# One layer of sparse attention and retention: values with v as stationary operand, gate projected transposed

## What is computed

```
u = rms_norm(x, norm_gain);  z = u @ w_in        # q k v gate of attention, index q k w, q k v gate of retention
score[t,s] = sum_h w_i[t,h] * relu(q_i[t,h] . k_i[s])      # causal; each query keeps its top 128 keys
p   = softmax(q_a . k_a / 8 over the kept keys)            # 8 heads of 64
y_a = (p @ v_a) * silu(g_a)
y_r = rms_norm_per_head(retention(q_r, k_r, v_r)) * silu(g_r)   # 4 heads, qk 64, v 128, chunks of 128
out = rms_norm(x + concat(y_a, y_r) @ w_out, final_gain)
```

## Time and profile before

| | us |
|---|---|
| median of three runs | 293.16 (292.93 to 293.17) |
| the profiled execution | 292.49 |
| its span from first to last instruction | 290.7 |

### The profile page before, as it was taken

One profiled execution on the slowest core, in us unless ns is written; L12 is line 12 of the kernel. 1 busy time (PEld: TensorE's weight loads), 2 busy tenths in 40 slices (PEclk: granted clock), 3 DMA queues, 4 the chain that ended last, 5 costly groups with the idle time before them and its releaser, 6 DMA issues.

```text
span 290.7 us, 4404 instructions
## 1 busy us (share of the span) xinstructions
PE 281.1 (97%) x1506; PEld 239.9 (83%) x1506; DVE 203.8 (70%) x414; ACT 142.8 (49%) x305; POOL 65.9 (23%) x122
## 2 busy tenths in 40 slices
PE   8999999999999999999999999999999999999991
PEld 7997888888888788877888888888888888888891
DVE  3967779999999999999956555658734733863341
ACT  5957646516455324582468442593444563341231
POOL 1016822132200068792400103011020020000211
PEclk9999999999999999999999999999999999999998
DMA  7998504210422043051303220212200407311123
GB/s 287 410 400 269 144 3 143 75 45 31 144 73 74 14 146 114 17 144 55 94 10 135 74 72 0 98 48 73 76 0 2 144 0 256 107 36 38 72 97 121
DMA packets 13845, 30.10 MB, mean 104 GB/s; under 512 B 1152, under 2 KB 1664, under 8 KB 13824
## 3 DMA queue, kind: packets, MB, share of 16 engines
q1 hardware_dynamic: 13248, 29.04, 30.3%
q10 hardware_dynamic: 576, 0.79, 0.7%
HBM read 27.73 MB, written 2.10 MB: 103 GB/s over the span
## 4 chain that ended last, share of the span: by engine, by line
PE 65%; DVE 20%; DMA 5%; issue 4%; POOL 2%; ACT 2%; SPq 2%; DVEq 0%; POOLq 0%; ACTq 0%
PE bank L441 16%; PE bank L443 15%; PE bank L442 15%; PE bank L492 6%; DVE keys L1079 6%; DVE top L1077 5%; DMA w_raw<-in_w_in 5%; DVE w_lo L978 3%; PE bank L506 3%; DVE keys L1064 2%; PE bank L521 2%; PE bank L522 2%; DVE k_stack L1040 2%; PE bank L531 1%; PE bank L552 1%
## 5 line engine op out<-in xcount | busy, mean ns | idle before, releaser
L441 PE MATMUL bank<-w_hi,xT_hi 128*128 128x512 f32 (+1 forms) x296 | 116.5, 394 | 0.6 <-DVE w_lo L978 0.5
L443 PE MATMUL bank<-w_hi,xT_lo 128*128 128x512 f32 (+1 forms) x296 | 114.1, 385 | 0.0
L442 PE MATMUL bank<-w_lo,xT_hi 128*128 128x512 f32 (+1 forms) x296 | 113.8, 384 | 0.0
L441 PEld LDWEIGHTS bank<-w_hi,xT_hi 128*128 128x128 f32 x296 | 55.7, 188 | 11.7 <-DVE w_lo L978 1.4
L443 PEld LDWEIGHTS bank<-w_hi,xT_lo 128*128 128x128 f32 x296 | 55.6, 188 | 11.5
L442 PEld LDWEIGHTS bank<-w_lo,xT_hi 128*128 128x128 f32 x296 | 55.7, 188 | 9.9
L978 DVE TENSOR_TENSOR w_lo<-w_raw,w_hi 128x1024 fp32r<-128x1024 f32 x36 | 45.2, 1276 | 16.3 <-ACT w_hi L622 16.1
L622 ACT ACTIVATE w_hi<-w_raw 128x1024 fp32r<-128x1024 f32 x36 | 37.4, 1053 | 5.7 <-PE bank L443 3.4
L737 ACT ACTIVATE work<-work,small 128x128 f32<-128x128 f32 (+3 forms) x32 | 17.8, 556 | 33.4 <-DVE small L1102 33.3
L1077 DVE MAX8 top<-keys 128x8 f32<-128x256 f32 (+2 forms) x48 | 26.9, 560 | 1.3
L916 POOL TENSOR_TENSOR th<-zt,tab 128x64 f32<-128x64 f32 (+1 forms) x24 | 13.1, 544 | 57.9 <-ACT zt L666 57.6
(11 more groups left out here) (130 smaller groups left out, 377.8 us busy)
## 6 DMA issues: line engine op xcount, KB each, us to landing
w_raw<-in_w_in SPq DMA_DIRECT2D x28, 512.0 KB, 3.8
w_raw<-in_w_out SPq DMA_DIRECT2D x8, 512.0 KB, 3.7
retT<-in_x SPq DMA_DIRECT2D x8, 256.0 KB, 3.7
x_h<-in_first SPq DMA_DIRECT2D x2, 836.0 KB, 7.8
out<-x_h SPq DMA_DIRECT2D x4, 320.0 KB, 2.5
v_ret<-in_x SPq DMA_DIRECT2D x2, 512.0 KB, 11.4
v_att<-in_x SPq DMA_DIRECT2D x2, 512.0 KB, 10.0
mix<-in_first SPq DMA_DIRECT2D x1, 836.0 KB, 5.4
```

Source lines behind the costliest of these rows:

```text
L441: pe.matmul(o, xh, hi[:, kk, c0:c0 + w], start=first, stop=False)
L442: pe.matmul(o, xh, lo[:, kk, c0:c0 + w], start=False, stop=False)
L443: mm = pe.matmul(o, xl, hi[:, kk, c0:c0 + w], start=False, stop=last)
```

## The change

- `values` takes v as the weights (64 columns) and the transposed probabilities as the moving operand (128 columns). The two heads of a pair go into partitions 0 to 63 and 64 to 127 of the bank, alternating for each key tile. Its result is y transposed.
- As the division by the sum can then no longer be made per row of the result, it is made on the probabilities: `reciprocal(s)` on VectorE for each pair, and `scale_probs(s)`, two copies with a scale on ScalarE. `transpose_probs(s)` waits for these.
- The chunks of the two gates change places: the gate of attention is now steps 24 to 27, that of retention 28 to 31.
- The gate of attention is projected transposed, with weights and x exchanged as operands, so its token factor is needed along the columns: `half_rstd` is spread by GpSimd, turned by four transposes in step 15 (`turn_rstd`) and copied by ScalarE. `att_z` multiplies it in on VectorE ahead of the tanh; `att_gate` makes the gate after the maximum.
- The y of blocks 0 and 1 is stashed in `qT` by ScalarE (`stash_y`) and gated in steps 28 and 29; blocks 2 and 3 are gated out of PSUM.
- `transpose_mix` has only the retention half; the attention half is already transposed. `retention_out` leaves the product with the gate to `ret_gate`, for chunks 0 to 2.
- On VectorE one top-k round of a step stands ahead of `reciprocal`, the others behind `retention_out`.

The diff, cut to its core:

```diff
 CHUNKS = [("idx", BASE, IDX_W), ("q", 0, ATT_W), ("k", ATT_W, ATT_W), ("v", 2 * ATT_W, ATT_W),
           ("ret_qk", BASE + IDX_W, 2 * RH * RQK),
           ("ret_v", BASE + IDX_W + 2 * RH * RQK, RH * RV),
-          ("ret_gate", BASE + IDX_W + 2 * RH * RQK + RH * RV, RH * RV),
-          ("att_gate", 3 * ATT_W, ATT_W)]
+          ("att_gate", 3 * ATT_W, ATT_W),
+          ("ret_gate", BASE + IDX_W + 2 * RH * RQK + RH * RV, RH * RV)]
 NCH = len(CHUNKS)
 CW = 512
 OUT_CH = D_MODEL // CW
...
         row_max = small[:, 20:22]
         neg_max = small[:, 22:24]
         den = small[:, 24:40].rearrange("p (b h) -> p b h", b=2)
...
+                    if c == C_AG:
+                        e = slice(m * P, (m + 1) * P)
+                        pe.matmul(o, hi[:, kk, e], xT_hi[:, k, :], start=first, stop=False)
+                        pe.matmul(o, lo[:, kk, e], xT_hi[:, k, :], start=False, stop=False)
+                        mm = pe.matmul(o, hi[:, kk, e], xT_lo[:, k, :], start=False, stop=last)
+                        continue
...
+            def turn_rstd():
+                pe.wait_ge(rstd_spread, 1)
+                pe.wait_ge(t_evac, 3 * MT)
+                pe.wait_ge(klo_done, MT)
+                for m in range(MT):
+                    mm = pe.transpose(mid_ps[:, m * P:(m + 1) * P], junk[:, m * P:(m + 1) * P], ident)
+                mm.then_inc(rstd_turned, 1)
...
-                if p == 0 and b >= 1:
-                    pe.wait_ge(y_att_psum, b)
-                for hh in range(2):
-                    h = 2 * p + hh
-                    pe.wait_ge(pt_evac, 2 * s + hh + 1)
-                    for j in range(b + 1):
-                        mm = pe.matmul(att_ps[:, h * HD:(h + 1) * HD], probT[:, hh, j * P:(j + 1) * P],
-                                       v_att[:, j, h * HD:(h + 1) * HD], start=(j == 0), stop=(j == b))
+                if p == 0 and 1 <= b <= STASHED:
+                    pe.wait_ge(y_stashed, b)
+                elif p == 0 and b > STASHED:
+                    pe.wait_ge(att_mixed, b)
+                pe.wait_ge(pt_evac, 2 * s + 2)
+                for j in range(b + 1):
+                    for hh in range(2):
+                        h = 2 * p + hh
+                        mm = pe.matmul(att_ps[64 * hh:64 * hh + 64, p * P:(p + 1) * P], v_att[:, j, h * HD:(h + 1) * HD],
+                                       probT[:, hh, j * P:(j + 1) * P], start=(j == 0), stop=(j == b))
                 mm.then_inc(pv_done, 1)
 
             def transpose_probs(s):
                 b = s // PAIRS
                 for hh in range(2):
-                    pe.wait_ge(exp_done, 2 * s + hh + 1)
+                    pe.wait_ge(p_scaled, 2 * s + hh + 1)
...
-                pe.wait_ge(att_mixed, m + 1)
                 pe.wait_ge(ret_mixed, m + 1)
                 pe.wait_ge(pt_evac, 2 * steps_before_mix(m))
-                for half in range(2):
-                    if m >= 1:
-                        pe.wait_ge(mixlo_done, 2 * (m - 1) + half + 1)
-                    for j in range(KH):
-                        e = (KH * half + j) * P
-                        mm = pe.transpose(trans_ps[half][:, j * P:(j + 1) * P], mix[:, m, e:e + P], ident)
-                    mm.then_inc(mixT_mm, 1)
+                if m >= 1:
+                    pe.wait_ge(mixlo_done, 2 * m)
+                for j in range(KH):
+                    e = ATT_W + j * P
+                    mm = pe.transpose(trans_ps[1][:, j * P:(j + 1) * P], mix[:, m, e:e + P], ident)
+                mm.then_inc(mixT_mm, 1)
...
+                if g == ATT0 - 1:
+                    turn_rstd()
...
-                    act.activation(th[:, :], src[:, :], ACT.Tanh, scale=half_rstd[:, m:m + 1]).then_inc(tanh_done, 1)
+                    if i < MT:
+                        act.wait_ge(az_done, i + 1)
+                        act.activation(th[:, :], attT[:, i, :], ACT.Tanh).then_inc(tanh_done, 1)
+                    else:
+                        act.activation(th[:, :], src[:, :], ACT.Tanh, scale=half_rstd[:, m:m + 1]).then_inc(tanh_done, 1)
...
-                    act.wait_ge(y_att_psum, b - 1)
+                    act.wait_ge(rden_done, PAIRS * (b - 1))
...
+            def scale_probs(s):
+                b = s // PAIRS
+                act.wait_ge(rden_done, s + 1)
+                for hh in range(2):
+                    pr = prob[:, hh, 0:cols(b)]
+                    act.activation(pr, pr, ACT.Copy, scale=rden[:, s % 2, hh:hh + 1]).then_inc(p_scaled, 1)
+            def stash_y(b):
+                act.wait_ge(pv_done, PAIRS * (b + 1))
+                act.wait_ge(q_lo_done, b + 1)
+                act.activation(qT[:, :, b * P:(b + 1) * P], att_ps[:, :].rearrange("p (a t) -> p a t", a=PAIRS),
+                               ACT.Copy).then_inc(y_stashed, 1)
...
+                act.wait_ge(att_mixed, m + 1)
+                act.activation(xT_hi[:, 0:KH, t], attT[:, :, t], ACT.Copy).then_inc(mixhi_done, 1)
+                act.wait_ge(mixT_mm, m + 1)
+                act.activation(xT_hi[:, KH:KT, t], trans_ps[1][:, :].rearrange("p (k t) -> p k t", k=KH),
+                               ACT.Copy).then_inc(mixhi_done, 1)
+            def rstd_row():
+                act.wait_ge(rstd_turned, 1)
+                act.activation(half_rstd_row[:, :], mid_ps[:, :], ACT.Copy).then_inc(rstd_row_done, 1)
...
+                if 0 <= g - ATT0 < STEPS:
+                    scale_probs(g - ATT0)
+                done = g - ATT0 - 2
+                if 0 <= done < PAIRS * STASHED and done % PAIRS == PAIRS - 1:
+                    stash_y(done // PAIRS)
...
+                if i == 3 * MT:
+                    pool.wait_ge(warmed, 1)
+                    pool.wait_ge(hrstd_done, 2)
+                    pool.tensor_copy(junk[:, :].rearrange("p (m t) -> p m t", m=MT), half_rstd.rearrange(
+                        "p (m t) -> p m t", t=1).broadcast_to([P, MT, P])).then_inc(rstd_spread, 1)
...
+            def att_z(n):
+                g = MT * C_AG + n
+                dve.wait_ge(proj_done, g + 1)
+                dve.wait_ge(rstd_row_done, 1)
+                dve.tensor_tensor(attT[:, n, :], proj_ps[g % 2][:, :], half_rstd_row[:, :], ALU.mult).then_inc(az_done, 1)
+            def att_gate(n):
+                dve.wait_ge(tanh_done, n + 1)
+                dve.scalar_tensor_tensor(out=attT[:, n, :], in0=th[:, :], scalar=1.0, in1=attT[:, n, :], op0=ALU.add,
+                                         op1=ALU.mult).then_inc(agate_done, 1)
...
+            def reciprocal(s):
+                b, p = s // PAIRS, s % PAIRS
+                dve.wait_ge(exp_done, 2 * s + 2)
+                if s >= 2:
+                    dve.wait_ge(p_scaled, 2 * (s - 1))
+                dve.reciprocal(rden[:, s % 2, :], den[:, b % 2, 2 * p:2 * p + 2]).then_inc(rden_done, 1)
...
             def attention_out(b):
 
...
+                if b == 0:
+                    dve.wait_ge(agate_done, MT)
+                t = slice(b * P, (b + 1) * P)
+                if b < STASHED:
+                    dve.wait_ge(y_stashed, b + 1)
+                    y = qT[:, :, t]
                 else:
-                    dve.wait_ge(*tmp_last_read[0])
-                    dve.tensor_tensor(tmp[:, :].rearrange("p (h d) -> p h d", h=HEADS), src, co, ALU.mult).then_inc(y_att_psum, 1)
-                    dve.wait_ge(y_att_psum, b + 1)
-                    dve.wait_ge(agate_psum, MT)
-                    dve.tensor_tensor(half, half, tmp[:, :], ALU.mult).then_inc(att_mixed, 1)
-                    tmp_last_read[0] = (att_mixed, MT)
+                    dve.wait_ge(pv_done, PAIRS * (b + 1))
+                    y = att_ps[:, :].rearrange("p (a t) -> p a t", a=PAIRS)
+                dve.tensor_tensor(attT[:, :, t], y, attT[:, :, t], ALU.mult).then_inc(att_mixed, 1)
...
                 dve.wait_ge(ret_step, 3 * n + 3)
-                if tmp_last_read[0]:
-                    dve.wait_ge(*tmp_last_read[0])
-                dve.tensor_tensor(tmp[:, :].rearrange("p (h d) -> p h d", h=RH),
-                                  mid_ps[:, :].rearrange("p (h d) -> p h d", h=RH),
-                                  rcoef.rearrange("p (h d) -> p h d", d=1).broadcast_to([P, RH, RV]),
-                                  ALU.mult).then_inc(y_ret_psum, 1)
+                half, y = mix[:, n, ATT_W:2 * ATT_W], mid_ps[:, :].rearrange("p (h d) -> p h d", h=RH)
+                co = rcoef.rearrange("p (h d) -> p h d", d=1).broadcast_to([P, RH, RV])
+                if n < MT - 1:
+                    dve.tensor_tensor(half.rearrange("p (h d) -> p h d", h=RH), y, co, ALU.mult).then_inc(y_ret_psum, 1)
+                    return
+                dve.wait_ge(*tmp_last_read[0])
+                dve.tensor_tensor(tmp[:, :].rearrange("p (h d) -> p h d", h=RH), y, co, ALU.mult).then_inc(y_ret_psum, 1)
                 dve.wait_ge(y_ret_psum, n + 1)
...
             def mix_lo(m):
-                for half in range(2):
```

(23 more changed lines are left out.)

83 lines of the change are left out of this document (36 added, 47 removed).

## The result

The changed kernel takes 303.41 us (median of 6 runs, 301.82 to 304.0) beside 293.05 us for the kernel before (6 runs, 292.5 to 293.38) on the same chip: ratio 1.0347, interval 1.0327 to 1.0368, so 3.5% slower. Its profiled execution took 301.82 us with a span of 300.0, against 290.7 before: +9.3 us in the traces.

The account below looks back on a forecast made before the run. TensorE, 97% busy, bounds the kernel. Its work -4.7, step 20 +3.2, retention loop and end +9.0 (10.0 less 1) give +7.5 on 292.49, so 300.0; with 0.67 for the median 300.7, called 300.5; range 291.5 to 304 us.

Parts of the forecast that it names:

- step 20: TensorE's scores(4) wait behind transpose_probs(3) for VectorE's top-k round and reciprocal and ScalarE's copies: +3.2 us, at least 2.3.
- TensorE's work: TensorE's own work on the path, from values, absorbed block 0 groups and mix transposes: -4.7 us.
- the clock: Rival: with TensorE waits of 3 us the clock might fall to 1.2 GHz for a stretch; over 304 us, chance 0.08.
- values: Half-array values groups on TensorE cost 0.35 + n x 0.055 us for n instructions: -2.6 us in all.
- block 0 absorbed, mix transposes: Extra cost of three block 0 values groups absorbed by the stall at 131 us, -0.5; 16 mix transposes fewer, -1.6 us.
- step 26: Retention loop: squares of chunk 0 come 1.4 us later against a cover of 0.95; TensorE waits 0.9 us.
- step 28: Retention loop: squares start 3.3 us later against TensorE, cover 0.6; TensorE waits 3.0 us.
- step 29: Retention loop: next_state(2) stands behind the delayed split; wait of 0.4 us.
- step 30: Retention loop: a delay of 3.7 us against a cover of 1.9; TensorE waits 2.3 us.
- step 33, `mix_lo(1)`: Output projection: mix_lo(1) stands behind retention_out(3), 2.1 us late, cover 0.9; TensorE waits 2.1 us.
- step 34, `mix_lo(2)`: mix_lo(2) stands behind the first residual add, whose x loads follow the last weight loads: wait of 1.3 us.
- main case: The waits as summed, slower, decided where a retention loop delay passes its cover: 297 to 304 us, chance 0.50.

Follow-up runs that it names:

- the filled kernel: The changed kernel with 12 dummy matmuls of 512 columns, result unread, ahead of TensorE's wait in step 28: 303.47 us, ratio 1.0376.

## Why the prediction was right

The sign and the mechanism hold: the scaling delays step 20 and uses up the cover of the retention loop, and TensorE waits there. The median is 2.9 us above the forecast of 300.5 and 0.6 under the upper end of its range, 304. That it lies no further off is in part luck, as terms of opposite sign were wrong: TensorE's work and step 20 came out 1.7 us better than I had them, and the clock 3.3 worse. The steps:

| Step | Forecast | Measured in the traces |
|---|---|---|
| values | -2.6 | -3.7 |
| block 0 absorbed, mix transposes | -0.5, -1.6 | -0.3; -1.2 is left for the transposes by the account's -5.2 (not measured by itself), where 16 at 0.1 us would be -1.6 |
| step 20 | +3.2 | +1.96 |
| step 26 | 0.9 | 1.17 |
| step 28 | 3.0 | 2.98 |
| step 29 | 0.4 | 0 |
| step 30 | 2.3 | 1.54 |
| step 31, `mix_lo(0)` | none | 1.63 |
| step 33, `mix_lo(1)` | 2.1 | 1.97, at the end of step 32 |
| step 34, `mix_lo(2)` | 1.3 | 0 |
| clock | 0 (a rival) | +3.3 |

**The values** were mis-sized by their fixed price: 0.35 us from `ret_kv`, 0.28 in place. The change of each group, put on what it took before (0.39, 0.84, 1.29, 1.74), gives 0.50, 0.73, 0.95 and 1.16 us for 4, 8, 12 and 16 instructions: 0.28 + 0.055 n. The pitch was exact; the trace shows it as pairs 0.006 us apart, one in each half, every 0.103 us. (My 0.107 for the old form was a little low: 12 more instructions took 1.35 us more, 0.112 each.) One part of the price depends on what comes behind: from this group of step 34 on, the next L452 has 0.34 us to L453 instead of 0.23.

```profile
259.03 0.39 PE L454 MATMUL bank<-w_hi,xT_lo 128*128 128x512 f32 x1
259.35 1.09 PE L516 MATMUL bank<-work,v_att 128*64 128x128 f32 x16
260.37 0.50 PE L452 MATMUL bank<-w_hi,xT_hi 128*128 128x512 f32 x1
260.71 0.40 PE L453 MATMUL bank<-w_lo,xT_hi 128*128 128x512 f32 x1
```

The Trainium skill, "TensorEngine Tiling (Array Packing)", Key Properties, has the drain as a rule without a figure; the 0.28 us is this trace's.

**Step 20** was mis-sized by VectorE's end of it. VectorE and ScalarE in the changed kernel:

```profile
129.66 1.13 DVE L1110 TENSOR_TENSOR q_lh<-qT,q_lh 64x512 fp32r<-64x512 f32 x1
130.82 0.69 DVE L1137 MAX8 top<-keys 128x8 f32<-128x512 f32 x1
...
132.22 0.15 DVE L1201 RECIPROCAL small<-small 128x2 f32<-128x2 f32 x1
```

```profile
132.41 0.69 ACT L773 ACTIVATE work<-work,small 128x128 f32<-128x128 f32 x2 [3.58 <-DVE small L1201]
```

I had the q remainder at up to 1.1 us past 131.31; it was done at 130.79, 0.5 us before, and so the delay came out under the lower bound of 2.3 us that I had put on it. VectorE stood for 0.61 us ahead of the first of its four operations (126.65), for ScalarE's rounding, so they began 0.5 us later than before and not 1.1: the three reciprocals went into a gap that I had not counted on. And the four took 4.14 us where they took 5.15 before (126.16 to 131.31). The chain behind them is as forecast (round, reciprocal, copies, transposes), with copies of 0.69 us instead of 0.44 and 0.5 us of transposes instead of 0.1.

The 1.0 us in those four operations came by chance. The same four take 0.69 us each in step 23, where GpSimd does nothing; in step 19 they run beside GpSimd's products and take 0.69 to 1.80 each, and GpSimd's take longer as well. Here are the first two of them in the changed kernel and in the filled one, whose program is the same up to step 28:

```profile
126.65 0.69 DVE L1110 TENSOR_TENSOR q_hl<-qT,q_hl 64x512 fp32r<-64x512 f32 x1 [0.61 <-ACT q_lh L744]
126.66 1.28 POOL L977 TENSOR_TENSOR tmp<-zt,tab 128x256 f32<-128x256 f32 x1
```

```profile
126.79 0.74 POOL L982 TENSOR_TENSOR tmp<-zt,tab 128x256 f32<-128x256 f32 x1
126.82 1.26 DVE L1115 TENSOR_TENSOR q_hl<-qT,q_hl 64x512 fp32r<-64x512 f32 x1 [0.60 <-ACT q_lh L749]
```

The engine that started first, by 0.01 and 0.03 us, kept its time and the other took 0.5 us more. In the filled kernel the four then took 5.25 us, ended at 132.07, and step 20's scores started at 134.68, 3.3 us later than in the kernel before: the term as I had forecast it. So the step-20 term came to 2.0 us in one trace and 3.3 in the other by which engine came first.

**The copies** were taken from PSUM copies of the same size; pairs from SBUF with a scale took 0.69 and 1.12 us for 128 and 384 columns where I had 0.44 and 0.87, 0.25 more for each pair. The scaling cost ScalarE 16.3 us instead of 12.2.

**Step 28** came out by its own parts. The squares start at 199.20 against 193.69 before, with TensorE 2.4 us later in that step, so 3.1 later against it (forecast 3.3), behind tanh, q rounding and the copies. First VectorE, then ScalarE:

```profile
197.97 0.17 DVE L1201 RECIPROCAL small<-small 128x2 f32<-128x2 f32 x1
202.27 0.69 DVE L1250 TENSOR_TENSOR mix<-bank,small 128x512 f32<-128x512 f32 x1 [4.14 <-POOL small L1020]
```

```profile
198.17 1.12 ACT L773 ACTIVATE work<-work,small 128x384 f32<-128x384 f32 x2 [0.43 <-DVE small L1201]
199.20 0.25 ACT L800 ACTIVATE junk<-bank 128x128 f32<-128x128 f32 x1
```

**Steps 31 to 34** were right in sum and wrong in place. I had put `mix_lo` against the next projection's start. With the attention half no longer transposed, `mix_lo(0)` and `mix_lo(1)` free the one bank that the second head's transposes of steps 31 and 32 need as well, and those come first. `mix_lo(0)` had no term at all. The delay was then paid, and step 34 had none: 5.14 us over steps 30 to 34 (1.54 + 1.63 + 1.97) where I had 5.7. That the sum fits is luck: one term was missing and one was for nothing. My 1.3 us for step 34 also rested on a misreading, as 244.97 comes 3.6 us after the end of the split (241.36) and 4.9 after its start.

**The clock** stood as a rival only, at 8%. It is the step that failed in the main case: waits of 3 us were in my own sum, and I let them cost no more than themselves. Of the sum of +7.5, TensorE's own work took off 0.5 more (-5.2 by the account), step 20 1.2 more, and the other waits put on 0.3 (9.3 for 9.0): that would have been +6.1. The clock's 3.3 makes it 9.4, against 9.3 seen. The median lies another 1 us further from that of before than the profiled executions do (10.4 against 9.3). No trace of those executions is there, so where it sits stays open; the 1.3 us by which step 20 differs between the changed and the filled kernel is a candidate.

## What to carry to other kernels

When a row-wise factor moves from behind a product to ahead of it, it becomes a wait between two engines in each step; price it by what else is queued on the engine that gets it, and move it between engines as their queues fill and empty. Here the same 32 operations with their reciprocals cost 14.3 us on ScalarE alone (+10.4 against -3.9 without them), 6.6 on VectorE alone and 1.4 when each took the steps in which it had room. Half-array matmuls pay only in groups long enough to carry 0.28 us of entry and exit, and most with the halves in turn. Once a forecast wait is 2 to 3 us long, a fall of the clock belongs among the terms, and with it the question whether a later wait takes it back.
